# The hidden values of a mixture-of-experts layer, turned by VectorE instead of TensorE

## The reference

```
def swiglu(h, wg, wu, wd):
    return einsum('...f,fd->...d', silu(h @ wg) * (h @ wu), wd)

for e in range(8):                      # wg, wu: 1024 x 2816; wd: 2816 x 1024
    out = out + dense_gate[:, e:e + 1] * swiglu(ht, wg[e], wu[e], wd[e])
```

## Time and profile before

| | us |
|---|---|
| median of 3 runs | 1406.71 (1405.79 to 1408.81) |
| the profiled execution | 1407.02 |
| its span in the profile | 1405.2 |
| TensorE busy | 1376.2 (98%) |
| VectorE busy | 510.9 (36%) |
| ScalarE busy | 382.5 (27%) |
| mean DMA rate over the span | 290 GB/s |

### The profile page before, as it was taken

The page is one execution under the profiler, slowest core; times in us unless marked ns, Lnnn a source line. Parts: engine busy times, 40 slices in busy tenths (PEclk is TensorE's granted clock), DMA queues, the critical chain, the costliest instruction groups (busy, mean ns, idle before and its releaser), DMA issues.

```text
span 1405.2 us, 33707 instructions
## 1 busy us (share of the span) xinstructions
PE 1376.2 (98%) x15380; PEld 947.3 (67%) x15380; DVE 510.9 (36%) x836; ACT 382.5 (27%) x519; POOL 73.2 (5%) x130
## 2 busy tenths in 40 slices
PE   6999999999999999999999999999989999999998
PEld 6779999888765545545445454464544579798896
DVE  6976545469661101001010010010101174657665
ACT  5665344256420000000000000000000156645653
POOL 3400000034010000000000000000000010000000
PEclk9999999999989999999999999999999999999999
DMA  9568875455759999999999999999999944333341
GB/s 330 173 229 296 291 265 200 128 163 169 268 211 391 380 391 409 398 387 400 400 406 395 394 396 408 386 403 385 407 355 371 380 140 164 120 122 131 109 180 61
DMA packets 122191, 407.18 MB, mean 290 GB/s; under 512 B 7046, under 2 KB 35574, under 8 KB 122052
## 3 DMA queue, kind: packets, MB, share of 16 engines
q1 hardware_dynamic: 113808, 389.57, 73.5%
q0 software_dynamic: 5408, 12.58, 2.7%
q10 hardware_dynamic: 2836, 2.88, 0.6%
HBM read 396.78 MB, written 16.12 MB: 294 GB/s over the span
## 4 chain that ended last, share of the span: by engine, by line
PE 87%; DVE 8%; ACT 2%; issue 1%; DMA 0%; SPq 0%; DVEq 0%; ACTq 0%
PE ps L2687 49%; PE ps L496 7%; PE ps L498 6%; PE ps L497 6%; DVE yT L2007 3%; PE ps L1179 2%; DVE low L486 2%; PE ps L1180 1%; PE ps L1181 1%; PE ps L2670 1%; PE ps L2359 1%; PE ps L2321 1%; PE ps L1386 1%; PE ps L1388 1%; PE ps L1387 1%
## 5 line engine op out<-in xcount | busy, mean ns | idle before, releaser
L2687 PE MATMUL ps<-ering,xe 128*32 128x384 f32 (+1 forms) x6144 | 462.1, 461 | 6.0 <-issue 6.0
L2687 PEld LDWEIGHTS ps<-ering,xe 128*32 128x32 f32 x6144 | 205.6, 110 | 256.7 <-issue 146.0
L2687 PE MATMUL ps<-ering,eT 128*32 128x256 f32 x4224 | 231.0, 379 | 0.0
L2183 DVE TENSOR_TENSOR eh<-eh,ps 128x384 f32<-128x384 f32 (+1 forms) x48 | 22.1, 517 | 540.1 <-PE ps L2687 540.1
L2687 PEld LDWEIGHTS ps<-ering,eT 128*32 128x32 f32 x4224 | 136.5, 110 | 91.0
L486 DVE TENSOR_TENSOR low<-raw,high 128x2048 fp32r<-128x2048 f32 (+3 forms) x48 | 128.8, 2686 | 61.5 <-ACT high L481 60.3
L481 ACT ACTIVATE high<-raw 128x2048 fp32r<-128x2048 f32 (+3 forms) x47 | 105.5, 2244 | 91.6 <-PE ps L498 76.1
L496 PE MATMUL ps<-high,xT_hi 128*128 128x352 f32 (+1 forms) x368 | 128.2, 348 | 1.2 <-DVE xT_lo L2089 1.2
L498 PE MATMUL ps<-high,xT_lo 128*128 128x352 f32 (+1 forms) x368 | 127.1, 345 | 0.0
L497 PE MATMUL ps<-low,xT_hi 128*128 128x352 f32 (+1 forms) x368 | 126.8, 345 | 0.0
L1861 ACT ACTIVATE eh<-ps 128x384 f32<-128x384 f32 (+1 forms) x48 | 18.8, 465 | 354.4 <-PE ps L2687 354.4
(11 more groups left out here) (436 smaller groups left out, 1669.7 us busy)
## 6 DMA issues: line engine op xcount, KB each, us to landing
ering<-in_moe_wd SPq DMA_DIRECT2D x48, 1536.0 KB, 11.3
ering<-in_moe_wg SPq DMA_DIRECT2D x32, 1536.0 KB, 8.7
ering<-in_moe_wu SPq DMA_DIRECT2D x32, 1536.0 KB, 11.3
ering<-in_moe_wg SPq DMA_DIRECT2D x32, 1280.0 KB, 11.4
ering<-in_moe_wu SPq DMA_DIRECT2D x32, 1280.0 KB, 11.1
rawb<-in_w_in SPq DMA_DIRECT2D x25, 1024.0 KB, 5.0
raw<-in_w_in SPq DMA_DIRECT2D x16, 1024.0 KB, 9.3
ering<-in_moe_wd SPq DMA_DIRECT2D x16, 1024.0 KB, 12.2
```

Source lines behind the costliest of these rows:

```text
L2687: mm = nc.tensor.matmul(out_of(rows), tokens, columns_of(s), start=begins, stop=ends, skip_group_check=True)
```

## The change

The strips' columns are taken in blocks of 32 in both pieces: strip s has every fourth block of 32 columns. A tile of 128 hidden indices then has 32 in each strip, and turning each 32x32 block where it stands (VectorE's `transpose`, STREAM_TRANSPOSE in the instruction list) puts all 128 on the partitions. VectorE does so from `eh` to `eT`, six times per item, right behind its multiplications; TensorE's `turn_hidden` and `turn_blocks` and VectorE's eight copies go. Chunk 12 now waits for the multiplications of piece 0, chunk 16 for the transposes of piece 0, and chunk 20 for those of piece 1. `turn_tokens` waits for ScalarE's last silu of the item as well. What is loaded, in what chunks and when SyncE may issue it, is unchanged.

```diff
-            def turned_tiles(i, jb): ...
-            def turned_blocks(i, n): ...
+            def turned(i, piece):
+                first, tiles = piece * WIDE[0] // STRIP, WIDE[piece] // STRIP
+                for t in range(TOKS):
+                    dve.wait_ge(emult_made, MULTS * i + 3 * piece + t + 1)
+                    nc.vector.transpose(eT[:, first:first + tiles, STRIP * t:STRIP * t + STRIP],
+                                        eh[piece][:, t, 0:WIDE[piece]].rearrange("p (b q) -> p b q", q=STRIP)).then_inc(et_made, 1)
...
             def turn_tokens(i):
                 pe.wait_ge(xg_landed, 16 * (i + 1))
+                pe.wait_ge(esilu_made, 6 * i + 6)
...
-            def columns_of(piece, w):
-                if piece == 0:
-                    return lambda s: w[:, WIDE[0] * s:WIDE[0] * s + WIDE[0]]
-                return lambda s: w.rearrange("p (b s q) -> p s b q", b=BLOCKS, s=STRIPS)[:, s, :, :]
+            def columns_of(w):
+                return lambda s: w.rearrange("p (b s q) -> p s b q", s=STRIPS, q=STRIP)[:, s, :, :]
...
                     if j == 12:
-                        pe.wait_ge(tp_freed, FREED * i + 3)
+                        pe.wait_ge(emult_made, MULTS * i + 3)
...
-                    if j == 8:
-                        turn_hidden(i)
-                        if first:
-                            turn_last_places()
+                    if j == 8 and first:
+                        turn_last_places()
...
-                    if j >= 20:
-                        pe.wait_ge(tp_freed, FREED * i + 3 + (DOWN_TILES[j - 16][-1] - 12) // 2 + 1)
+                    if j in (16, 20):
+                        pe.wait_ge(et_made, TURNS * i + (3 if j == 16 else 6))
...
                     mm.then_inc(w_used, 1)
-                    if j == 16:
-                        turn_blocks(i)
-                        if not last:
-                            turn_tokens(i)
+                    if j == 16 and not last:
+                        turn_tokens(i)
```

More of the change, by code:

```diff
@@ L55 @@
 PIECE0 = STRIPS * WIDE[0]
-HALF = P // 2
-BLOCKS = WIDE[1] // HALF
 ESLOTS = 8
@@ L394, in model_program @@
     tp_filled, tp_freed = sem("tp_filled"), sem("tp_freed")
-    esilu_made, emult_made = sem("esilu_made"), sem("emult_made")
+    esilu_made, emult_made, et_made = sem("esilu_made"), sem("emult_made"), sem("et_made")
     PAIR = (0, 1)
@@ L537, in model_program @@
     LAST_BANKS = ((2, 3, 4, 5), (0, 1, 6, 7))
-    FILLS, FREED, MULTS = 8, 10, 6
+    FILLS, FREED, MULTS, TURNS = 2, 2, 6, 6
     Y_ISSUE = (2, 7, 12, 16)
@@ L2204, in item @@
                     dve.wait_ge(xs_landed, 16 * 2 * NB)
-                for jb in range(3):
-                    turned_tiles(i, jb)
+                turned(i, 0)
                 if first:
@@ L2213, in item @@
                 hidden(i, 1)
-                for n in range(BLOCKS):
-                    turned_blocks(i, n)
+                turned(i, 1)
                 if last:
@@ L2220, in item @@
                 for part in range(2):
-                    dve.wait_ge(tp_filled, FILLS * i + 6 + part + 1)
+                    dve.wait_ge(tp_filled, FILLS * i + part + 1)
                     nc.vector.tensor_copy(xe[:, 4 * part:4 * part + 4, :],
@@ L2654, in turn_tokens @@
                     mm.then_inc(tp_filled, 1)
[L2656 to L2674, removed]
             def turn_last_places():
@@ L2688, in by_strips @@
                 return mm
-            def columns_of(piece, w):
-                if piece == 0:
-                    return lambda s: w[:, WIDE[0] * s:WIDE[0] * s + WIDE[0]]
-                return lambda s: w.rearrange("p (b s q) -> p s b q", b=BLOCKS, s=STRIPS)[:, s, :, :]
+            def columns_of(w):
+                return lambda s: w.rearrange("p (b s q) -> p s b q", s=STRIPS, q=STRIP)[:, s, :, :]
             def out_of(piece, bank):
-                if piece == 0:
-                    return lambda rows: ps[rows, bank, 0:WIDE[0]]
-                return lambda rows: ps[rows, bank, 0:WIDE[1]].rearrange("p (b q) -> p b q", b=BLOCKS)
+                return lambda rows: ps[rows, bank, 0:WIDE[piece]].rearrange("p (b q) -> p b q", q=STRIP)
             def gate_or_up(j):
@@ L2706, in gate_or_up @@
                     for t in range(TOKS):
-                        mm = by_strips(out_of(piece, 3 * up + t), xe[:, kt, STRIP * t:STRIP * t + STRIP], columns_of(piece, w[:, k, :]),
+                        mm = by_strips(out_of(piece, 3 * up + t), xe[:, kt, STRIP * t:STRIP * t + STRIP], columns_of(w[:, k, :]),
                                        kt == 0, kt == KT - 1)
```

## The result

The changed kernel takes 1396.55 us, the median of 4 runs (1394.22 to 1400.08), against 1406.25 us for the kernel before on the same chip (4 runs): a ratio of 0.993, 95% interval 0.9917 to 0.9943. In a second comparison it took 1395.22 us (5 runs, 1392.54 to 1396.09) against 1406.59 (9 runs): 0.9916 (0.9903 to 0.993). It is faster by 10 to 11 us. The forecast was 1385.4 us, a gain of 21.6, and the range ended at 1396.0. So about half of the gain did not come. The first time is just outside the range and the second just inside it; on which side of its end the time falls is chance, since the range ended where a rival with another mechanism stood.

What follows compares the result with a forecast made beforehand. TensorE was taken to bound the kernel, the DMA close behind. Removed turns save 26.7 us, waits for loads return 5.1, so 1407.0 - 21.6 = 1385.4 us; own range 1383 to 1390, full range 1379.8 to 1396.0.

Steps and rivals of the forecast that it cites:

- What bounds it: Items of the mixture: TensorE's chain of 89.40 us an item bounds, never waiting for a load; the DMA has little to spare.
- no gain: Rival: the loads already set 89.4 us an item and TensorE's chain only looks full; within 0.2% of 1407.0 us, chance 0.03.
- What leaves TensorE: Removed turning groups on TensorE, before chunks 9 and 17: 3.34 us saved an item, 26.7 us over 8 items.
- The lower bound, 3.03: Least saving on TensorE from the removed groups, by the chain of waits: 3.03 us an item, or 24.2 us.
- Runs of 32 columns, VectorE's transposes, the new waits: Replacements on TensorE and VectorE: short operand runs taken as free, transposes and waits finished long before they are needed.
- The rival on the slower side: Rival: runs of 32 columns slow gate and up chunks by 10%, +45.4 us against -26.7, 1425.7 us; chance 0.07.
- The waits for loads: Items 4 to 6: TensorE uses up its 11.6 us lead, then waits for loads, taken as 5.1 us in all.
- The DMA gains at most its idle shares up to there ... together 5 us: Up to item 6, a more eager TensorE wins idle DMA time: 1.6 us, then about 0.7 in each of five stretches.
- 9.7 us if none of the idle share is won: Items 4 to 6: upper value for TensorE's waits for loads, against 4.7 us with the idle share won.
- Item 7 and the end: Item 7 judged safe: its 5.41 us pause remains, loads catch up and stay a few us ahead to the end.
- The signs that I had named: Items at about 86 us first, 88 to 89 in items 5 and 6; loads landing after over 15 us; gate chunk 3.87.
- The loads bind harder: Rival: deeper queues win nothing and loads take 1% longer, saving 11.7 us, 1395.3 us, or 1396.2 with clock dips; chance 0.14.

Runs made afterwards that it cites:

- the loads by themselves: Changed kernel with two of three token groups left out of the gate and up products, so TensorE never holds up a load: 1394.27 us.
- the turns put back: Changed kernel with TensorE's two groups of turning products put back, their output read by nobody: 1405.79 us, 0.9994 of the kernel before.
- the two profiles: Two profiled executions of the unedited changed kernel: the first took 1400.08 us, the second 1396.09 us.
- faster loads alone: Changed kernel with the next item's tokens loaded to 128 partitions instead of 96: 1385.1 us, 0.9848 of the kernel before.
- the other order alone: Changed kernel with ScalarE's last result copies moved ahead of the third rounded load of the second block: 1394.71 us, 0.9904 of the kernel before.
- both together: Changed kernel with tokens loaded to 128 partitions and ScalarE's last result copies moved earlier: 1382.2 us, 0.9829 of the kernel before.
- wide tokens and loads alone: Changed kernel with two of three token groups left out of the gate and up products and tokens loaded on 128 partitions: 1383.57 us.

## Why the prediction was wrong

*What bounds it: right for the kernel before.* TensorE in front, the DMA close behind. It was closer than I had put it, as the loads by themselves need 89.85 us an item against TensorE's 89.40, so that the gain was limited to the lead. The rival "no gain" is out, by that lead.

*What leaves TensorE: right, a little large.* 3.34 us an item were forecast from the releases of chunks; the chain's 89.40 - 86.24 = 3.16 us is what came, 25.3 us over 8 items and not 26.7. The lower bound, 3.03, was as near.

*Runs of 32 columns, VectorE's transposes, the new waits: right.* Nothing, by the turns put back. The rival on the slower side falls with that.

*The waits for loads: the right mechanism, too small.* The step that failed is "The DMA gains at most its idle shares up to there ... together 5 us". It gained nothing. Loads alone need 89.85 us an item where I had put 88.6, since an idle share averaged over 16 engines is not idle time of the slowest: the last part of item 3's last load arrived at 746.8 us before and after the change. My own other end, "9.7 us if none of the idle share is won", lies between the 10.7 and 7.5 us of the two profiles. I had placed the value at 5.1 "because more loads are always queued once TensorE is eager". More loads were queued, with 20.8 us from issue to landing, and the landings came no earlier; only the parts of a load came further apart. Per load the waits were under 2 us and did not lower the clock, as forecast.

*Item 7 and the end: wrong, and the larger part.* "The first loads of the second block (`rawb`) queue behind and keep some 3 us of lead" was said of the loads against TensorE's first need of them. I did not follow who else stands behind these loads. On ScalarE it is the copy of the last expert results, and that engine's slack before was 4.7 us while I forecast TensorE to come 21.6 us earlier. The trace of before had the row with that slack. Given back: 10.3 - 2.7 = 7.5 us in the one profile, 10.1 - 2.7 = 7.4 in the other. Two causes share it, as the table of the end shows: faster loads alone bring the 10.3 us to 7.1, the other order alone to 5.4, and both together to 2.8, the 2.7 of before, without idle time.

The sum for the second profile: -25.3 by TensorE, +7.5 waits for loads and +7.4 at the end make -10.4; its span is 10.9 us shorter than before. For the first: -25.3 + 10.7 + 7.5 = -7.1, and the span is 6.9 shorter. (The pause before item 7, longer by 0.7 and 0.6 us, is left out of both.) The forecast was -26.7 + 5.1 = -21.6. Of the 11.2 us between it and the second profile's sum, 1.4 are TensorE's term, 2.4 the loads and 7.4 the end.

*The signs that I had named.* The items of 86 us at first, the unchanged gate chunk, the transposes of 0.43 to 0.50 us, the loads of over 15 us to landing, the waits that end with a load and the nearly unchanged pause came as said. Items 5 and 6 took 90.45 and 90.22 us (89.59 and 90.37 in the second profile) instead of 88 to 89: the sign of the term that was too small. No sign was named for the end of the mixture.

*The rivals.* "The loads bind harder" gave 1395.3, nearly the measured time, by luck. It puts 26.7 - 11.7 = 15.0 us on waits for loads, where 10.7 and 7.5 came; its lowered clocks did not come with these waits (granted clock 1.00 from 760 to 935 us); and the end of the mixture, which fills the difference, it does not mention. (Its saving of 17.1 us is 26.7 - 9.7 = 17.0.)

## What to carry to other kernels

When an engine gets earlier by x us, look at the stage's end for every instruction that is in a fixed order behind a load, on all engines, and note its slack; where it is under x a part of the gain ends there. Here it cost nothing to put the copies that release the next stage ahead of work prepared for later. A mean DMA share just under 1 is no reserve: ask how long the loads take with nothing to wait for, and measure it by thinning out the compute. Once the loads bind, look for the odd transfer among them: here 384 KB on 96 partitions cost 2.8 us each, and making it a third larger was worth 10 us.

## What the hardware showed that I had not expected

- A load on 96 partitions between loads on 128 cost three times its bytes (2.8 us for 0.96), and the load widened to 128 partitions just its bytes (1.25 us). In the changed kernel the window 869 to 878, with such a reload in flight, has a share of 1.01 at 323 GB/s; with the wide reload the same window has 394. The kernel before has such stretches too, and the trace that I predicted from shows that a full share does not mean a full rate, here from 700 to 705 us:

```profile
700.00:705.00 5.00, 5.00 (x68) 2.06 (x64) 0.00 (x0) 0.00 (x0) 0.00 (x0) 1.00 1.01 318
```

  Why the reload costs that much stays open; that different engines serve the 96 partitions, as I had supposed, is not shown.
- The arrival of one load's 16 parts can spread over 13 us where loads take over 20 us from issue to landing, and it stays within 4 us where they take 11. It also grows with the wide reload and without any, so the reload is not its cause. Which engine is slow, and why, was not tried.
- With deep queues the issue itself can block SyncE. The reload's issue took 0.34 us in items 1 and 2 of the changed kernel, then 0.70, 3.79 and 8.31, and 0.34 again in item 6. Item 5, on SyncE's timeline:

```profile
859.89 8.31 SPq L1542 DMA_DIRECT2D xg<-xs  x1
868.39 9.08 SPq L456 DMA_DIRECT2D ering<-in_moe_wu  x3
```

  With wide tokens and loads alone it reaches 9.2 us too, so the 96 partitions are not its cause; how much is queued probably is, which no run varies by itself.
- A product whose moving operand is read in twelve or ten runs of 32 columns takes the time of an unbroken one: 490 ns for 384 columns either way.
